# Copies of old cache rows issued in the last stage of a decoder step instead of the first

## The chip, the core and the metric

The kernel runs on one core of one Trainium2 chip. The metric is the device time of one execution in microseconds. Engines are named as in the profile: PE is TensorE, PEld its weight load, DVE is VectorE, ACT is ScalarE, POOL is GpSimd, SP is SyncE, which here only issues DMAs. HBM holds inputs and outputs.

## What is computed

One step of a decoder layer for a prompt of 2048 tokens and for 8 sequences of 4 new tokens each. The changed part is the last output of this cut of the reference: the rolling windows of keys and values, 2048 rows of 512 floats (2 KB) for each of 8 sequences. The first 2044 rows are old rows of the input, moved up by four; the last four are the new ones.

```
qa, ka, va, qb, kb, vb = project_qkv(rmsnorm(hs, norm_attn[l]), w_in[l], pos_s)
lb = state_win_k.shape[2]
k_all = jnp.concatenate([state_win_k[l], ka], axis=1)
v_all = jnp.concatenate([state_win_v[l], va], axis=1)
...
hs = hs + mix.astype(hs.dtype) @ w_out[l]
hs = mlp_sublayer(hs, norm_mlp[l], w_up[l], w_down[l])
...
wk_s.append(k_all[:, t:t + lb])
wv_s.append(v_all[:, t:t + lb])
```

Nothing in the kernel reads the old rows from the output: attention takes them from the input.

## The kernel before

Four stages run one after the other, each a block that all engines leave together through a barrier: `project`, `attend_prompt`, `attend_decode`, `mlp`. Every engine runs its own list of instructions in order, and semaphores tie the lists together.

**`project`** makes two passes (`h` = 0, 1) over 17 tiles of 128 tokens (the last has 32). Each pass has three column groups of the input weights in SBUF, split into a high and a low part, and each tile is multiplied three times per group (lines 398 to 400). For a tile, ACT squares `x` (line 253), DVE scales it by the root (line 303, which counts `xs_ready`), PE turns it (line 379) and multiplies, ACT copies the result, DVE rotates it (lines 345 to 350), PE turns it again (line 409), and ACT and DVE split the turned result (lines 287, 361). SP issues, in this order, the load of `x` for the tile after the next (line 164), the stores of keys and values (line 198), and four stores of 256 KB of the turned queries and keys (line 210: `qT_hi`, `qT_lo`, `kT_hi`, `kT_lo`). Between the passes SP loads the other three groups of weights (line 170), ACT casts them to the high part (line 263), and POOL subtracts to get the low part (line 239).

POOL also copies the old rows. `copy_window(n)` issues four DMAs from HBM to HBM for sequence `n`, a body of 2032 rows (4064 KB) and a rest of 12 rows, for keys and for values (lines 231, 233), once `xs_ready` has reached 3n + 5, so one sequence every three tiles. Four sequences come ahead of the subtractions of line 239, four behind them. POOL then waits for all of them.

**`attend_prompt`** and **`attend_decode`** are not touched. In `attend_decode` POOL issues 512 loads of cached values (line 843), among DVE's copies of turned keys (line 1086).

**`mlp`** goes over 5 blocks `b` of 416 tokens. A block first takes 8 column tiles of the output projection, then 16 groups `g` of hidden features. In a group PE multiplies two column tiles of the up weights, ACT and DVE apply the squared relu and split the result, and PE multiplies the down weights of the group before; DVE adds each of the eight results into `y` (line 1728), which frees one of three PSUM banks `d_dps`. All weights are read from HBM again for each block and split on the way: SP loads a tile to a raw buffer (line 1315 up, 512 KB; line 1320 down, 1024 KB), ACT casts it to the high part (lines 1514, 1520), and DVE subtracts (lines 1670, 1663). There are two raw buffers for up weights and one for down weights; DVE's subtraction lets SP issue the next load:

```
def load_rows(b, g):
    wait(sp, down_lo_ready, row_no(b, g))
    src = io["w_down"].rearrange("(g f p) n -> g p f n", p=P, f=NF)[g]
    sp.dma_start(down_raw[:], src).then_inc(down_in, 16)
```

Here `row_no(b, g)` is `b * 16 + g`. SP also loads the next block's mixed heads in some groups (line 1330) and stores the finished rows (line 1353). POOL has nothing to do in this stage.

Of the kernel before, what the change touches and what calls it, by code (L numbers as in the profile page):

```python
# [27 lines left out]
ND, TD = 8, 4  # L28
# [5 lines left out]
WIN = 2048  # L34
# [36 lines left out]
def project(nc, io, keep):  # L71
# [8 lines left out]
    NG, NR = 3, 2  # L80
# [3 lines left out]
    with ExitStack() as ctx:  # L84
        sb = lambda n, s, d=F32: ctx.enter_context(nc.sbuf_tensor(n, s, d))
        ps = lambda n: ctx.enter_context(nc.psum_tensor(n, [P, 512], F32))
        sem = lambda n: ctx.enter_context(nc.semaphore(n))
# [23 lines left out]
        w_ready = [sem(f"a_w_ready{i}") for i in range(2)]  # L111
# [4 lines left out]
        xs_ready = sem("a_xs_ready")  # L116
# [9 lines left out]
        stored = [sem(f"a_stored{b}") for b in range(2)]  # L126
        vec = sem("a_vec")
        VEC = 2 * NR + 1 + 2
        copied = sem("a_copied")

        w_cols = io["w_in"].rearrange("(c p) (g n) -> g p c n", p=P, n=GW)
        name = lambda h, i: GROUPS[i] + "ab"[h]
# [25 lines left out]
        with nc.Block() as block:  # L158
# [61 lines left out]
            @block.gpsimd  # L220
            def _(pool):

                body = (WIN - TD) // 16 * 16
                pool.wait_ge(w_ready[0], NG)

                def copy_window(n):
                    pool.wait_ge(xs_ready, n * 3 + 5)
                    for k in ("ka", "va"):
                        src = io[k + "_state"][bass.ds(n, 1)].rearrange("o t n -> (o t) n")
                        dst = io[k + "_win"][bass.ds(n, 1)].rearrange("o t n -> (o t) n")  # L230
                        pool.dma_start(dst[0:body].rearrange("(a b) n -> a b n", a=16),
                                       src[TD:TD + body].rearrange("(a b) n -> a b n", a=16)).then_inc(copied, 16)
                        pool.dma_start(dst[body:WIN - TD], src[TD + body:WIN]).then_inc(copied, 16)

                with pool.Fori(0, ND // 2) as n:
                    copy_window(n)
                for i in range(NG):
                    pool.wait_ge(w_hi_ready, NG + i + 1)
                    nc.gpsimd.tensor_tensor(w_lo[i][:], w_raw[(NG + i) % 2][:], w_hi[i][:].bitcast(F32),
                                            ALU.subtract).then_inc(w_ready[1], 1)  # L240
                with pool.Fori(ND // 2, ND) as n:
                    copy_window(n)
                pool.wait_ge(copied, 16 * 4 * ND)

            @block.scalar
            def _(act):
# [972 lines left out]
def mlp(nc, io, keep):  # L1219
# [3 lines left out]
    NB = (S + NS) // W  # L1223
# [3 lines left out]
    OG, UG = KC, FF // (NF * P)  # L1227
# [5 lines left out]
    with ExitStack() as ctx:  # L1233
        sb = lambda n, s, d=F32: ctx.enter_context(nc.sbuf_tensor(n, s, d))
        ps = lambda n: ctx.enter_context(nc.psum_tensor(n, [P, 512], F32))
        sem = lambda n: ctx.enter_context(nc.semaphore(n))
# [35 lines left out]
        down_hi_ready, down_lo_ready = sem("d_down_hi_ready"), sem("d_down_lo_ready")  # L1272
# [14 lines left out]
                                                   sem("d_y_rooted"))  # L1287
        y_ready = sem("d_y_ready")
        stored = [sem(f"d_stored{i}") for i in range(2)]
        vec = sem("d_vec")  # L1290

        out_no = lambda b, c: b * CG + c
# [12 lines left out]
        with nc.Block() as block:  # L1305
            @block.sync
            def _(sp):
# [77 lines left out]
                    put(LAST, t)  # L1385
                for i in range(2):
                    sp.wait_ge(stored[i], 16 * (NB * TB // 2 + (i == (NB * TB - 1) % 2)))

            def three(dst, w_hi, w_lo, x_hi, x_lo, first, last):

                nc.tensor.matmul(dst, w_hi, x_hi, start=first, stop=False)  # L1391
                nc.tensor.matmul(dst, w_hi, x_lo, start=False, stop=False)  # L1392
                return nc.tensor.matmul(dst, w_lo, x_hi, start=False, stop=last)  # L1393
# [400 lines left out]
def build(nc, io):  # L1794
    with ExitStack() as ctx:
        sb = lambda n, s: ctx.enter_context(nc.sbuf_tensor(n, s, F32))
        keep = {"ident": sb("ident", [P, P]), "qsT": sb("qsT", [P, 2 * NP, NS]), "ksT": sb("ksT", [P, 2 * NP, NS]),
                "mixsT": sb("mixsT", [P, 2 * NP, NS]), "neg_lam": sb("neg_lam", [P, 1])}
        for name in ("qT_hi", "qT_lo", "kT_hi", "kT_lo", "mixT"):
            io[name] = nc.dram_tensor(name, [2 * NP, P, S], F32, kind="Internal").ap()  # L1800
        project(nc, io, keep)
        attend_prompt(nc, io, keep)
        attend_decode(nc, io, keep)
        mlp(nc, io, keep)
# [91 lines left out]
```

## Time and profile before

| | before |
|---|---|
| median of 3 runs | 4207.3 us (4205.71 to 4209.13) |
| the profiled execution, own time | 4212.42 us |
| span of the profiled execution | 4210.9 us |
| granted clock of PE, mean | 0.961 |
| PE busy | 3851.8 us, 91% of the span |
| DVE busy | 2363.2 us, 56% |
| ACT busy | 1663.2 us, 39% |
| POOL busy | 921.5 us, 22% |
| DMA, mean | 172 GB/s, 722.35 MB in 493617 packets |
| `mlp`, from 2459 us on: PE busy | 1696.25 of 1752 us |
| `mlp`: DMA share, rate | 0.41, 123 GB/s |

The span runs from the first to the last instruction; the execution's own time has a little around it. Busy shares are means over stages with different limits, so each stage has to be read by itself. A granted clock of 1.00 is the upper of PE's two levels (2.4 GHz), 0.50 the lower (1.2 GHz). The DMA share is the mean busy share of the core's 16 DMA engines; it can come out a little over 1 in short stretches.

### The profile page before, as it was taken

To read this page: it belongs to the slowest core of one execution; us is meant where nothing else is said; L and a number is where in the kernel's file an instruction comes from. 1 tells how busy PE (TensorE), PEld (TensorE's weight loads), DVE (VectorE), ACT (ScalarE), POOL (GpSimd) and SP (SyncE) were. 2 spreads that over 40 slices of the span, in tenths; PEclk is the share of its full clock that TensorE was granted. 3 is DMA by queue.
4 is the path that set the end of the run, shared out by engine and by line. 5 is a ranking of instruction groups with operands and counts; after the bars stand their busy time and mean duration, and the time that the engine had idled before them with its cause. 6 is when DMAs were issued, how large, how long until landed. Compare 5 with 4: busy or idle time off the path is not lost. (4 is left out here: it accounts for less than half of the span.)

```text
span 4210.9 us, 72902 instructions
## 1 busy us (share of the span) xinstructions
PE 3851.8 (91%) x25066; PEld 3178.3 (75%) x25066; DVE 2363.2 (56%) x4793; ACT 1663.2 (39%) x2919; POOL 921.5 (22%) x784
## 2 busy tenths in 40 slices
PE   7997797999999978888888869999999999999998
PEld 6885685676777754444444549999999999999998
DVE  4344332555577854434434446666676676776765
ACT  2222121666666643222222234434444444443442
POOL 0002000988855543333333300000000000000000
PEclk9998998999999989989998979999999999999999
DMA  5776764111111129989989954334434433443432
GB/s 178 259 251 211 240 197 140 57 61 61 61 61 61 66 84 386 356 318 340 341 327 330 351 153 147 114 106 147 137 115 134 136 114 119 145 125 105 140 120 67
DMA packets 493617, 722.35 MB, mean 172 GB/s; under 512 B 30512, under 2 KB 331696, under 8 KB 487889
## 3 DMA queue, kind: packets, MB, share of 16 engines
q1 hardware_dynamic: 444841, 499.03, 36.5%
q0 software_dynamic: 47488, 218.01, 14.4%
q8 instruction: 191, 3.13, 0.3%
q14 instruction: 161, 1.32, 0.1%
q10 hardware_dynamic: 936, 0.86, 0.1%
HBM read 650.15 MB, written 134.48 MB: 186 GB/s over the span
## 5 line engine op out<-in xcount | busy, mean ns | idle before, releaser
L546 POOL TENSOR_SCALAR b_w<-b_w,b_inv 128x128 f32<-128x128 f32 (+7 forms) x192 | 578.9, 3025 | 425.8 <-DVE b_inv L698 255.4
L1728 DVE TENSOR_TENSOR d_y<-d_y,d_dps 128x416 f32<-128x416 f32 x640 | 372.2, 586 | 246.6 <-PE d_dps L1393 246.6
L1391 PE MATMUL d_dps<-d_u_hi,d_down_hi 128*128 128x416 f32 x1280 | 458.6, 358 | 11.4 <-DVE d_y L1728 11.4
L1393 PE MATMUL d_dps<-d_u_hi,d_down_lo 128*128 128x416 f32 x1280 | 453.1, 354 | 0.0
L1393 PE MATMUL d_ups<-d_h_hi,d_up_lo 128*128 128x416 f32 x1280 | 451.8, 353 | 0.0
L1391 PE MATMUL d_ups<-d_h_hi,d_up_hi 128*128 128x416 f32 x1280 | 449.9, 352 | 0.0
L1392 PE MATMUL d_dps<-d_u_lo,d_down_hi 128*128 128x416 f32 x1280 | 448.4, 350 | 0.0
L1392 PE MATMUL d_ups<-d_h_lo,d_up_hi 128*128 128x416 f32 x1280 | 446.7, 349 | 0.0
L898 PE MATMUL c_turn<-ident,c_k 128*128 128x128 f32 x2304 | 362.4, 297 | 69.5 <-ACT c_kT L1025 35.4
L898 PEld LDWEIGHTS c_turn<-ident,c_k 128*128 128x128 f32 x2304 | 262.0, 148 | 199.3 <-ACT c_kT L1025 88.0
L843 POOL DMA_DIRECT2D c_v<-in_v_cache x512 | 276.1, 539 | 596.2 <-issue 596.2
L622 ACT ACTIVATE b_w<-b_w,b_shift 128x128 f32<-128x128 f32 (+15 forms) x256 | 309.0, 1207 | 131.9 <-DVE b_shift L691 130.3
L398 PE MATMUL a_zps<-a_w_hi,a_xT_hi 128*128 128x512 f32 (+1 forms) x816 | 330.2, 405 | 10.6 <-DVE a_w_lo L331 7.5
L400 PE MATMUL a_zps<-a_w_hi,a_xT_lo 128*128 128x512 f32 (+1 forms) x816 | 326.7, 400 | 0.0
L399 PE MATMUL a_zps<-a_w_lo,a_xT_hi 128*128 128x512 f32 (+1 forms) x816 | 324.8, 398 | 0.0
L593 PE MATMUL b_ops<-b_wT,b_v 128*64 128x128 f32 (+1 forms) x3264 | 304.5, 282 | 21.9 <-ACT b_wT L634 17.4
L1086 DVE COPY c_kT<-c_turn 128x512 f32<-128x512 f32 x288 | 199.3, 692 | 202.8 <-PE c_turn L898 202.7
L1670 DVE TENSOR_TENSOR d_up_lo<-d_up_raw,d_up_hi 128x1024 fp32r<-128x1024 f32 x200 | 244.0, 1221 | 96.3 <-ACT d_up_hi L1514 96.2
L593 PEld LDWEIGHTS b_ops<-b_wT,b_v 128*64 128x64 f32 (+1 forms) x3264 | 250.8, 156 | 60.5 <-ACT b_wT L634 28.7
L1025 ACT COPY c_kT<-c_turn 128x512 f32<-128x512 f32 x288 | 168.7, 586 | 318.1 <-PE c_turn L898 318.1
L634 ACT COPY b_wT<-b_turn 128x512 f32<-128x512 f32 (+3 forms) x416 | 206.8, 522 | 156.0 <-PE b_turn L577 154.8
L577 PE MATMUL b_turn<-ident,b_w 128*128 128x128 f32 x1632 | 248.0, 285 | 18.0 <-POOL b_w L546 8.8
(188 smaller groups left out, 6849.9 us busy)
## 6 DMA issues: line engine op xcount, KB each, us to landing
c_k<-in_k_cache SPq DMA_DIRECT2D x512, 256.0 KB, 7.0
c_v<-in_v_cache POOLq DMA_DIRECT2D x512, 256.0 KB, 5.8
d_up_raw<-in_w_up SPq DMA_DIRECT2D x160, 512.0 KB, 4.2
d_down_raw<-in_w_down SPq DMA_DIRECT2D x80, 1024.0 KB, 5.5
out_ka_win<-in_ka_state POOLq DMA_DIRECT2D x8, 4064.0 KB, 15.8
out_va_win<-in_va_state POOLq DMA_DIRECT2D x8, 4064.0 KB, 27.6
d_up_raw<-in_w_out SPq DMA_DIRECT2D x40, 512.0 KB, 3.9
a_x<-in_x_prompt SPq DMA_DIRECT2D x32, 512.0 KB, 5.0
```

The source lines that it names most:

```text
L398: nc.tensor.matmul(dst, x_hi, w_hi[i][:, c, :], start=(c == 0), stop=False)
L399: nc.tensor.matmul(dst, x_hi, w_lo[i][:, c, :], start=False, stop=False)
L400: m = nc.tensor.matmul(dst, x_lo, w_hi[i][:, c, :], start=False, stop=(c == KC - 1))
L546: nc.gpsimd.tensor_scalar(row, row, inv[:, u % RB, m:m + 1], None, ALU.mult).then_inc(w_ready, 1)
L593: ins = nc.tensor.matmul(bank[h, at], v[i][:, kt, h], wT[copy_no(u, j, m) % WB][:, kt % 4 * P:(kt % 4 + 1) * P], start=(kt == 0), stop=(kt ...
L622: nc.scalar.activation(row, row, ACT.Exp, bias=shift[:, u % RB, m:m + 1], scale=-1.0, accum_out=total[:, u % RB, m:m + 1]).then_inc(exp_do ...
L843: eng.dma_start(dst[i][:, g, :], io[src[0]][bass.ds(page, 1)].rearrange("o p d -> (o p) d")).then_inc(landed[i], 16)
L898: last = nc.tensor.transpose(turn[e % 2][:, g * P:(g + 1) * P], k[i][:, half * 4 + g, p * P:(p + 1) * P], keep["ident"][:])
L1391: nc.tensor.matmul(dst, w_hi, x_hi, start=first, stop=False)
L1392: nc.tensor.matmul(dst, w_hi, x_lo, start=False, stop=False)
L1393: return nc.tensor.matmul(dst, w_lo, x_hi, start=False, stop=last)
L1728: nc.vector.tensor_tensor(part, part, d_ps[k % DB][:, 0:W], ALU.add).then_inc(d_used, 1)
```

## The change

The copies of the old rows leave `project`, and with them the counter `copied` and POOL's waits there. POOL gets a list in `mlp` instead. For each of the 80 groups (5 blocks of 16) it waits until DVE has split the group's down weights (`down_lo_ready`, line 1663 of the kernel before) and issues one copy of 400 rows (800 KB); behind every fifth piece it issues the remaining 44 rows of that window (88 KB). At the end POOL waits for all 96.

```diff
--- before.py
+++ after.py
@@ -126,7 +126,6 @@
         stored = [sem(f"a_stored{b}") for b in range(2)]
         vec = sem("a_vec")
         VEC = 2 * NR + 1 + 2
-        copied = sem("a_copied")
 
         w_cols = io["w_in"].rearrange("(c p) (g n) -> g p c n", p=P, n=GW)
         name = lambda h, i: GROUPS[i] + "ab"[h]
@@ -220,27 +219,10 @@
             @block.gpsimd
             def _(pool):
 
-                body = (WIN - TD) // 16 * 16
-                pool.wait_ge(w_ready[0], NG)
-
-                def copy_window(n):
-                    pool.wait_ge(xs_ready, n * 3 + 5)
-                    for k in ("ka", "va"):
-                        src = io[k + "_state"][bass.ds(n, 1)].rearrange("o t n -> (o t) n")
-                        dst = io[k + "_win"][bass.ds(n, 1)].rearrange("o t n -> (o t) n")
-                        pool.dma_start(dst[0:body].rearrange("(a b) n -> a b n", a=16),
-                                       src[TD:TD + body].rearrange("(a b) n -> a b n", a=16)).then_inc(copied, 16)
-                        pool.dma_start(dst[body:WIN - TD], src[TD + body:WIN]).then_inc(copied, 16)
-
-                with pool.Fori(0, ND // 2) as n:
-                    copy_window(n)
                 for i in range(NG):
                     pool.wait_ge(w_hi_ready, NG + i + 1)
                     nc.gpsimd.tensor_tensor(w_lo[i][:], w_raw[(NG + i) % 2][:], w_hi[i][:].bitcast(F32),
                                             ALU.subtract).then_inc(w_ready[1], 1)
-                with pool.Fori(ND // 2, ND) as n:
-                    copy_window(n)
-                pool.wait_ge(copied, 16 * 4 * ND)
 
             @block.scalar
             def _(act):
@@ -1287,6 +1269,7 @@
                                                    sem("d_y_rooted"))
         y_ready = sem("d_y_ready")
         stored = [sem(f"d_stored{i}") for i in range(2)]
+        rows_copied = sem("d_rows_copied")
         vec = sem("d_vec")
 
         out_no = lambda b, c: b * CG + c
@@ -1385,6 +1368,25 @@
                     put(LAST, t)
                 for i in range(2):
                     sp.wait_ge(stored[i], 16 * (NB * TB // 2 + (i == (NB * TB - 1) % 2)))
+
+            @block.gpsimd
+            def _(pool):
+
+                rows, pieces = 400, NB
+                rest = WIN - TD - rows * pieces
+                for n in range(NB * UG):
+                    pool.wait_ge(down_lo_ready, n + 1)
+                    who, k = n // pieces, n % pieces
+                    state = ("ka", "va")[who % 2]
+                    src, dst = io[state + "_state"][who // 2], io[state + "_win"][who // 2]
+                    at = slice(k * rows, (k + 1) * rows)
+                    old = slice(TD + k * rows, TD + (k + 1) * rows)
+                    pool.dma_start(dst[at].rearrange("(a b) n -> a b n", a=16),
+                                   src[old].rearrange("(a b) n -> a b n", a=16)).then_inc(rows_copied, 16)
+                    if k == pieces - 1:
+                        pool.dma_start(dst[WIN - TD - rest:WIN - TD].rearrange("(a b) n -> a b n", a=4),
+                                       src[WIN - rest:WIN].rearrange("(a b) n -> a b n", a=4)).then_inc(rows_copied, 16)
+                pool.wait_ge(rows_copied, 16 * (NB * UG + 2 * ND))
 
             def three(dst, w_hi, w_lo, x_hi, x_lo, first, last):
```

On POOL, in the projection, the order before was this (the three subtractions stand once, between two loops of four turns each):

```order
L235 ISA
L231 ISA [waits a_xs_ready]
L231 DMA out_ka_win<-in_ka_state 64x16256
L233 ISA
L233 DMA out_ka_win<-in_ka_state 16x384
L231 DMA out_va_win<-in_va_state 64x16256
L233 DMA out_va_win<-in_va_state 16x384
L235 REGISTER_ALU
L235 COMPARE_AND_BRANCH
L239 ISA
L239 TENSOR_TENSOR a_w_lo<-a_w_raw,a_w_hi 128x4096 [waits a_w_hi_ready] x3
L241 UNCONDITIONAL_BRANCH
```

and it is this now, in the numbering of the changed kernel:

```order
L219 UNCONDITIONAL_BRANCH [waits barrier_Pool_Activation_PE_DVE_SP_gather]
L224 ISA
L224 TENSOR_TENSOR a_w_lo<-a_w_raw,a_w_hi 128x4096 [waits a_w_hi_ready] x3
L157 UNCONDITIONAL_BRANCH
L521 UNCONDITIONAL_BRANCH [waits barrier_Pool_Activation_PE_DVE_SP_gather]
```

Only the subtractions are left between the two barriers; a body went out as 64 runs of 16256 floats.

On POOL, at the start of the last stage, where there was no row before, there now stands:

```order
L1372 UNCONDITIONAL_BRANCH [waits barrier_Pool_Activation_PE_DVE_SP_gather]
L1384 DMA out_ka_win<-in_ka_state 16x12800 [waits d_down_lo_ready] x5
L1387 DMA out_ka_win<-in_ka_state 16x1408
L1384 DMA out_va_win<-in_va_state 16x12800 [waits d_down_lo_ready] x5
L1387 DMA out_va_win<-in_va_state 16x1408
```

and so on for 16 windows: five pieces of 16 runs of 12800 floats, then a rest. The order of the instructions on PE, DVE, ACT and SP is the same as before.

## Rows read from the trace of the kernel before

**Rows 1.** Busy time by stretch: PE, PEld, DVE, ACT, POOL (instructions), granted clock, DMA share, GB/s.

```profile
250.00:300.00 50.00, 50.00 (x237) 40.82 (x236) 20.93 (x46) 11.49 (x23) 1.99 (x4) 1.00 0.86 283
...
400.00:450.00 50.00, 27.31 (x124) 22.25 (x123) 11.20 (x26) 4.48 (x9) 0.00 (x0) 0.80 0.96 316
450.00:500.00 50.00, 50.00 (x237) 40.82 (x236) 19.88 (x45) 11.38 (x23) 1.99 (x4) 1.00 0.69 229
```

**Rows 2.** Timeline of POOL, projection: start, us, operation, idle time before.

```profile
383.59 0.71 POOL L231 DMA_DIRECT2D out_ka_win<-in_ka_state  x1
...
397.10 0.50 POOL L231 DMA_DIRECT2D out_ka_win<-in_ka_state  x1 [11.33 <-DVE a_xs L303]
```

**Rows 3.** Timeline of SP's queue, projection, tiles with and without copies.

```profile
163.61 10.95 SPq L210 DMA_DIRECT2D kT_lo<-a_zT_lo  x1
...
394.93 23.76 SPq L210 DMA_DIRECT2D kT_hi<-a_zT_hi  x1
418.79 17.02 SPq L210 DMA_DIRECT2D kT_lo<-a_zT_lo  x1
436.07 2.46 SPq L164 DMA_DIRECT2D a_x<-in_x_prompt  x1
...
456.64 0.68 SPq L210 DMA_DIRECT2D kT_lo<-a_zT_lo  x1
```

**Rows 4.** Waits, 290 to 460 us: engine, what it waited for, sum, times, longest.

```profile
ACT a_xs L253 <- DMA a_x<-in_x_prompt: 31.3, 2, 30.5
```

**Rows 5.** Timeline of PE, first row after the stall.

```profile
445.65 1.75 PE L379 MATMUL a_turn<-ident,a_xs 128*128 128x128 f32 x7 [22.69 <-DVE a_xs L303]
```

**Rows 6.** Timeline of DVE, line 303, three tiles.

```profile
395.61 0.76 DVE L303 TENSOR_SCALAR a_xs<-a_x,a_stat 128x1024 f32<-128x1024 f32 x1
...
456.98 0.76 DVE L303 TENSOR_SCALAR a_xs<-a_x,a_stat 128x1024 f32<-128x1024 f32 x1
...
475.55 0.76 DVE L303 TENSOR_SCALAR a_xs<-a_x,a_stat 128x1024 f32<-128x1024 f32 x1
```

**Rows 7.** Busy time by stretch, just after the stall.

```profile
445.00:450.00 5.00, 4.35 (x17) 3.87 (x18) 4.35 (x11) 0.49 (x1) 0.00 (x0) 0.65 0.68 234
```

**Rows 8.** Source lines in the decode stage: min/median/max ns, first and last start.

```profile
L843 POOL DMA_DIRECT2D c_v<-in_v_cache x512: 538/539/601, 1566.2 to 2437.2; - x171
...
L1086 DVE COPY c_kT<-c_turn x288: 691/692/693, 1566.4 to 2439.2; 128x512 f32<-128x512 f32 x144
```

**Rows 9.** Page, part 6, DMA issues: KB each, median us to landing.

```profile
d_up_raw<-in_w_up SPq DMA_DIRECT2D x160, 512.0 KB, 4.2
d_down_raw<-in_w_down SPq DMA_DIRECT2D x80, 1024.0 KB, 5.5
...
out_va_win<-in_va_state POOLq DMA_DIRECT2D x8, 4064.0 KB, 27.6
```

**Rows 10.** Timelines of SP and of ACT in one group of the last stage.

```profile
3438.81 0.37 SPq L1315 DMA_DIRECT2D d_up_raw<-in_w_up  x1
3441.02 0.37 SPq L1320 DMA_DIRECT2D d_down_raw<-in_w_down  x1
...
3449.65 1.04 ACT L1514 CAST d_up_hi<-d_up_raw 128x1024 fp32r<-128x1024 f32 x1
3452.60 1.91 ACT L1520 CAST d_down_hi<-d_down_raw 128x2048 fp32r<-128x2048 f32 x1 [1.91 <-PE d_dps L1393]
```

**Rows 11.** Timeline of SP, a group that also loads the mix.

```profile
3250.70 0.37 SPq L1330 DMA_DIRECT2D d_mix<-mixT  x1
```

**Rows 12.** Busy time by stretch, the same group.

```profile
3240.00:3260.00 20.00, 20.00 (x103) 19.52 (x102) 13.65 (x21) 8.73 (x16) 0.00 (x0) 0.91 0.47 144
```

**Rows 13.** Waits of PE, last stage from 2560 us.

```profile
PE d_dps L1391 <- DVE d_y L1728: 11.4, 5, 2.6
```

**Rows 14.** Source line 345 on DVE: min/median/max ns.

```profile
L345 DVE TENSOR_TENSOR a_rot<-a_z,a_cos x68: 278/292/7061, 39.6 to 707.7; 128x128 f32<-128x128 f32 x64, 32x128 f32<-32x128 f32 x4
```

**Rows 15.** Timeline of DVE, the last split of down weights.

```profile
4167.63 2.29 DVE L1663 TENSOR_TENSOR d_down_lo<-d_down_raw,d_down_hi 128x2048 fp32r<-128x2048 f32 x1 [1.40 <-ACT d_down_hi L1520]
```

## The prediction

> **What bounds the kernel now.** I read the busy time by stretches first, since the change takes work out of one stage and puts it into another; then the waits and the timelines of the one stretch of the first stage in which TensorE stands idle while copies fly; then a group of the last stage, action by action. TensorE is the engine to look at in both stages.
>
> In the projection TensorE is busy for 50.00 of 50 us while the copies run beside it: from 250 to 300 us, with the DMA engines at a share of 0.86. The stretch from 400 to 450 us is different: 27.31 us busy, granted clock 0.80, and a DMA share of 0.96. From 450 us it is full again [rows 1]. So eight copies of K and eight of V cost this stage nothing most of the time, and something once.
>
> What happens there is a chain of five rows. POOL issues one pair of copies at 383.59 us and the next at 397.10 us, 13.5 us apart [rows 2], where the loops mean them to come three tiles apart. POOL had stood in the three subtractions of line 239 in between, so a pair that was due earlier came out late, just ahead of the next. With four bodies of 4064 KB on their way, SP's queue takes no more: the store of `kT_hi` sits 23.76 us in its issue and the one of `kT_lo` 17.02 us, where the latter takes 0.68 us with no copy in flight and 10.95 us beside one pair [rows 3]. Behind them in the same queue stands the load of `x` for the next tile; it is issued at 436.07 us. ScalarE's square of that tile waits 30.5 us for it [rows 4], and TensorE's turn of the tile is idle for 22.69 us [rows 5]. One pair at a time is absorbed, because the load is needed only a tile later; two are not.
>
> **The change, part by part.** *The copies leave the projection.* SP's stores are then issued in under 1 us each, as without a copy [rows 3], and the load of `x` goes out at about 396 us in place of 436 us, a whole tile before it is wanted. What that is worth comes from the pace of the tiles. Line 303 makes the normalized `x`, once a tile: at 395.61 us, then late, and two and three tiles on at 456.98 and 475.55 us [rows 6]. The steady distance is 475.55 - 456.98 = 18.57 us. Undisturbed, the start of 475.55 us would have stood at 395.61 + 3 x 18.57 = 451.32 us. The difference is **24.2 us**. A second way agrees: 22.69 us of idle time, and after it the clock is 0.65 for 4.35 us of work [rows 7], which loses (1 - 0.65) x 4.35 = 1.5 us, 24.2 together. TensorE also stands idle ahead of 383.59 us, during the reload of the weights and the subtractions on POOL; these stay, no copy flies beside them, and I count nothing for it. The gain reaches the end undiminished, as the later stages start at a barrier and depend on none of this.
>
> The largest that this term could be is ScalarE's whole wait, 30.5 us; the smallest is nothing, if the store queue were full for another reason.
>
> *POOL's wait for the copies at the end of the projection goes.* The last pair goes out when 7 x 3 + 5 = 26 of the 34 tiles have been normalized, eight tiles of 18.57 us before the stage's end, and lands in two. Worth nothing.
>
> *80 copies of 800 KB come into the last stage, and 16 rests of 88 KB.* POOL has no other work there, so its 96 issues (about 0.5 us each by the rows of the decode stage [rows 8]) delay nobody on POOL itself. The cost would be in what the transfers do to SP's weight loads. Two times 4064 KB are down 27.6 us after the second was issued [rows 9], so 800 KB are 800 / 8128 x 27.6 = 2.7 us of all DMA engines. A piece is let go by `down_lo_ready`, the same event that lets SP issue the next down weights, so the two do collide, in each of the 80 groups.
>
> The slack to set against it: in a typical group SP issues a load of up weights at 3438.81 us and one of down weights at 3441.02 us. They land after 4.2 and 5.5 us at the median [rows 9], so at 3443.0 and 3446.5 us. ScalarE casts these very tiles at 3449.65 and 3452.60 us, and the second cast waited for TensorE [rows 10]. So both have 6.1 to 6.6 us to spare, against 2.7 us (3.0 us where a rest follows). The second up load of the group has more. Nearest to the change there is a row that already does the like: at 3250.70 us SP adds an 832 KB load of `d_mix` to a group's own loads [rows 11], and TensorE is busy 20.00 of 20 us there [rows 12]. Over the whole of the stage from 2560 us on, TensorE's longest sum of waits is 11.4 us in five places, for additions on VectorE [rows 13]; no row there names a DMA. I take **0 us**. The bounds: nothing is won here by any row, as TensorE has no DMA wait to lose; on the other side I allow that the five waits for VectorE double, 11.4 us.
>
> *POOL's issue beside VectorE.* A copy is issued when line 1663 ends on VectorE, and line 1670 begins there at once. Rows of the decode stage: 512 POOL issues of 538 to 601 ns, and among them 288 copies on VectorE that took 691 to 693 ns, none of them stretched [rows 8]. But the row of line 345 shows that the two engines can block each other: 278 to 292 ns as a rule, and 7061 ns once, beside POOL's subtraction [rows 14]. I take the decode rows as the nearer ones, since a DMA issue is what POOL does here: 0 us. The Trainium skill ("SBUF — State Buffer", section "Who interferes with whom") says that VectorE and GpSimd share one pair of SBUF ports by an exclusive lock, that an instruction with two SBUF inputs contends with a GpSimd instruction that reads SBUF, and that the writing of descriptors can be shut out by some forms on VectorE. The trace agrees with the lock at line 345; for a DMA issue beside an instruction with two SBUF inputs no run here shows either. By that rule the sum would lie between this forecast and the first rival below.
>
> *The end.* The last piece is let go when the last line 1663 ends, at 4167.6 + 2.3 = 4169.9 us [rows 15], 41 us before the end of the span. Even with the 27.6 us of a whole copy in place of 3 us it would land before the last stores. The new wait at the end of POOL costs nothing.
>
> **The sum.** -24.2 + 0 + 0 + 0 = -24.2 us. The profiled execution took 4212.42 us around its span of 4210.9 us, 5.1 us above the median of 4207.3 us; its span should become about 4186.7 us. Taken off the median: 4207.3 - 24.2 = **4183 us**, 0.58% less. A measurement of this kernel tells about 0.2% from no change, 8.4 us.
>
> **Rivals.**
>
> *VectorE and POOL block each other in the last stage (slower).* Each of the 96 issues falls on an instruction of VectorE and holds it for about 0.5 us, and TensorE, which needs VectorE's additions to free its three `d_dps` banks, waits as long: 96 x 0.5 = 48 us, so 4183 + 48 = 4231 us. For it: line 345, and that VectorE's line 1670 starts just as POOL does. Against it: the 288 unstretched copies, and that VectorE is idle for 6.35 of 20 us even in a loaded stretch [rows 12], so that a delay of 0.5 us is made up within the group. It decides from the point where more than half of the 0.5 us reaches TensorE in each group (above 0.25 x 96 = 24 us the gain is gone).
>
> *The weight loads come late (slower).* If the copy's long runs pushed the loads back by the 10.95 us that one pair gave to `kT_lo` [rows 3], that is 10.95 - 6.6 = 4.3 us past the slack; times 80 it is 344 us, near 4530 us. It decides from a delay of over 6.6 us. Against it: that pair was ten times the bytes, and a piece of 2.7 us of service can't hold a queue for 11 us.
>
> *Nothing changes.* SP's queue was full of its own stores after the reload of the weights, the stall stays, and the time is 4207 us. For it: the stores come in a burst as TensorE starts again after the reload. Against it: the same store takes 0.68 us at a tile without copies and 10.95 us beside one pair [rows 3].
>
> That the change doesn't do what it says can be left aside: the rows of POOL's order show the copies gone from the first stage and 80 + 16 of them in the last.
>
> **How the numbers follow.** The forecast: 0.86. Nothing changes: 0.07. Blocked VectorE: 0.04. Late loads: 0.03. The forecast is the only case over 0.2% faster, the two slow ones are the slower cases: 0.86, 0.07, 0.07. The range is the forecast's own: down to the whole of ScalarE's wait (4207.3 - 30.5, about 4176), up to the doubled waits in the last stage (4183 + 11.4, about 4195). The 14% of the rivals and a little of the forecast's own lie outside.
>
> **What would show it.** Right: from 400 to 450 us TensorE is busy for 50 us at clock 1.00; SP's `kT_hi` and `kT_lo` issues are all below 1.5 us; the projection ends about 24 us earlier and the stages behind it keep their lengths; DMA share of the last stage goes from 0.4 to 0.5, and TensorE's waits there stay near 11 us. Wrong: a TensorE wait on `d_up_lo` or `d_down_lo`, a ScalarE wait for `d_up_raw` or `d_down_raw`, lines 1670 or 1728 (two lines further on in the new numbering) longer than before, or a `kT_hi` issue of tens of us that is still there.

## The result and the profile after

The changed kernel took **4183.5 us** (median of 5 runs, 4176.7 to 4189.8) against 4208.4 us for the kernel before (5 runs, 4205.7 to 4216.0): a ratio of 0.9938, 95% interval 0.992 to 0.9957. A repeat gave 0.9941 (0.9923 to 0.9959). The forecast was 4183 us, 0.9942. The profiled execution took 4177.45 us around its span of 4175.8 us.

First, the stretch of the projection in which TensorE stood idle. By stretches (columns as in [rows 1]):

```profile
250.00:300.00 50.00, 50.00 (x240) 40.90 (x239) 18.52 (x42) 11.75 (x24) 0.00 (x0) 1.00 0.38 113
400.00:450.00 50.00, 50.00 (x241) 40.94 (x241) 22.05 (x48) 11.37 (x23) 0.00 (x0) 1.00 0.33 104
450.00:500.00 50.00, 50.00 (x237) 40.85 (x236) 19.91 (x47) 9.15 (x18) 0.00 (x0) 1.00 0.35 111
```

And SP's queue at the tile that was stuck before:

```profile
392.74 0.41 SPq L209 DMA_DIRECT2D kT_hi<-a_zT_hi  x1
393.25 0.64 SPq L209 DMA_DIRECT2D kT_lo<-a_zT_lo  x1
394.15 0.66 SPq L163 DMA_DIRECT2D a_x<-in_x_prompt  x1
```

The two stores are issued in 0.41 and 0.64 us where they took 23.76 and 17.02 us [rows 3]; the load of `x` goes out at 394.15 us, where it went at 436.07 us. TensorE's 27.31 busy us of 50 [rows 1] are 50.00, at clock 1.00. Of TensorE's waits for line 303 (now 285) between 290 and 460 us, the 22.69 us [rows 5] are gone; one of 10.4 us stays, at the reload of the weights:

```profile
PE a_turn L361 <- DVE a_xs L285: 10.4, 1, 10.4
```

Second, the last stage, from the last matmul of the decode stage to the end of the span: 1751.8 us before, 1758.0 us after.

```profile
2417.80:4175.80 1758.00, 1698.52 (x9012) 1664.13 (x9012) 1171.92 (x1570) 726.78 (x1061) 46.74 (x96) 0.98 0.50 161
```

The same stretch before:

```profile
2459.10:4210.90 1751.80, 1696.15 (x9012) 1661.97 (x9012) 1171.71 (x1570) 726.08 (x1061) 0.00 (x0) 0.98 0.41 123
```

POOL's 96 issues are there and the DMA share went from 0.41 to 0.50, but the stage is 6.2 us longer. The transfers of the page (KB each, median us to landing):

```profile
d_up_raw<-in_w_up SPq DMA_DIRECT2D x160, 512.0 KB, 4.8
d_down_raw<-in_w_down SPq DMA_DIRECT2D x80, 1024.0 KB, 7.1
out_ka_win<-in_ka_state POOLq DMA_DIRECT2D x40, 800.0 KB, 6.9
out_va_win<-in_va_state POOLq DMA_DIRECT2D x40, 800.0 KB, 6.9
```

The weights land 0.6 and 1.6 us later than in [rows 9]. Two waits answer to [rows 13], here from 2520 us on; the second was not there before:

```profile
PE d_dps L1393 <- DVE d_y L1730: 14.4, 5, 3.7
ACT d_up_hi L1516 <- DMA d_up_raw<-in_w_up: 3.3, 4, 1.6
```

A fifth wait of ScalarE for these weights, 0.5 us, lies just ahead of 2520 us; so there is one at the start of each of the five blocks.

Where the time went, stage by stage in the profiles. The projection ends with TensorE's last turn of `z`, the second stage is from its first score to its last output matmul, the decode stage from its first turn of a key to its last `c_x` matmul, the last stage from there to the end of the span; the 18 to 20 us between the first and the second, and between the second and the third, are left out.

```
us                projection ends   second stage   decode   last stage   span
before                713.0            814.3        894.7     1751.8    4210.9
after                 686.7            811.1        882.5     1758.0    4175.8
after, repeat         686.6            809.4        878.1     1757.5    4169.1
before, repeat        711.1            814.0        901.0     1751.3    4216.1
```

The projection's end and the last stage move with the change and repeat within 2 us. The decode stage differs by 4 to 23 us between these four, though nothing in it was changed. So the difference of the two spans, 35.1 us, can't be read as the gain; the stages that the change touches give -26.3 + 6.2 = -20 us, and the medians -24.9 us.

### The profile page after: what moved, and what is told of

Its sections match the earlier page's. It is cut to its first block and busy times, and to the rows that moved or that the text cites. A ratio compares the mean times of both kernels' runs of the same rounds, so it can differ in the third digit from the quotient of the medians.

```text
span 4175.8 us, 72858 instructions
## 1 busy us (share of the span) xinstructions
PE 3846.3 (92%) x25066; PEld 3174.9 (76%) x25066; DVE 2363.1 (57%) x4793; ACT 1663.1 (40%) x2919; POOL 952.2 (23%) x848
## 5 line engine op out<-in xcount | busy, mean ns | idle before, releaser
L1393 PE MATMUL d_dps<-d_u_hi,d_down_hi 128*128 128x416 f32 x1280 | 459.7, 359 | 14.4 <-DVE d_y L1730 14.4
```

## The experiments

The theory, A in the texts on record: two pairs of copies in flight at once stop SP's queue, and this alone is the stall; in the last stage the copies are nearly covered. Its rivals are named in each text: that any copy in the projection costs, that nothing was gained there, that VectorE and POOL block each other in the last stage, or that the weight loads come late in every group. Each kernel was timed in rounds against the kernel before on the same chip; the ratios have 95% intervals.

**No copies at all.** From the changed kernel, the POOL block of `mlp` is taken out:

```diff
-            @block.gpsimd
-            def _(pool):
-
-                rows, pieces = 400, NB
...
-                pool.wait_ge(rows_copied, 16 * (NB * UG + 2 * ND))
```

> The changed kernel without the 96 copies in the last stage; the old rows of the windows are left out of the output. Theory A (the gain comes from the projection alone, and the copies in the last stage cost a few us at the five block starts): the projection as long as in the changed kernel (last turn of z at about 687 us), VectorE's additions hold TensorE up for 11.4 us in all in the last stage again (14.4 us with the copies), time 3 to 6 us below the changed kernel, 0.992 to 0.993 of the kernel before. Rival B (the copies cost nothing at all where they are now): the same time as the changed kernel, 0.994, and 14.4 us of waits stay.

Measured: 4174.4 us, ratio 0.9927 (0.9905 to 0.9949). The projection ends at 688.1 us and the last stage takes 1750.3 us. TensorE's five waits for `d_y` are down to 11.3 us, which speaks against rival B; the times alone can't tell the two apart. What the copies still cost in the changed kernel thus shows in the last stage, 6 to 8 us.

**Only the two pairs that collide.** From the kernel before, the first loop is taken out and the second issues two pairs; the other six are left out:

```diff
-                with pool.Fori(0, ND // 2) as n:
-                    copy_window(n)
...
-                with pool.Fori(ND // 2, ND) as n:
+                with pool.Fori(ND // 2, ND // 2 + 2) as n:
                     copy_window(n)
-                pool.wait_ge(copied, 16 * 4 * ND)
+                pool.wait_ge(copied, 16 * 4 * 2)
```

> The kernel before with only the fifth and sixth pair of copies left, issued behind the three subtractions as before; the other six sequences' old rows are left out of the output. Theory A (these two pairs, close together, make the whole stall): SP's kT_hi and kT_lo issues stay at 24 and 17 us, TensorE's wait for the turn stays at about 22.7 us, ratio to the kernel before 1.000 (within 0.002). Rival C (all copies slow the projection a little, and the stall is only a part): at least 5 us faster than the kernel before.

Measured: 4200.9 us, ratio 0.999 (0.9974 to 1.0007). The projection ends at 711.0 us. SP's queue, first the stuck stores:

```profile
392.92 23.71 SPq L210 DMA_DIRECT2D kT_hi<-a_zT_hi  x1
416.73 16.17 SPq L210 DMA_DIRECT2D kT_lo<-a_zT_lo  x1
433.15 2.46 SPq L164 DMA_DIRECT2D a_x<-in_x_prompt  x1
```

and TensorE's waits for line 301:

```profile
PE a_turn L377 <- DVE a_xs L301: 32.2, 2, 21.7
```

Two pairs of eight make the whole stall (the sum of 32.2 us holds the 10.4 us of the reload as well). The other six pairs add nothing to the projection's end: 711.0 us without them, 713.0 and 711.1 us with them. The times alone don't exclude rival C, as the interval reaches down to 0.9974, 11 us.

**All eight pairs, but kept apart.** From the kernel before; the second loop waits for one window's tiles more, so that the pair that POOL is late with doesn't meet the next:

```diff
-                def copy_window(n):
-                    pool.wait_ge(xs_ready, n * 3 + 5)
+                def copy_window(n, late=0):
+                    pool.wait_ge(xs_ready, n * 3 + (5 + late))
...
                 with pool.Fori(ND // 2, ND) as n:
-                    copy_window(n)
+                    copy_window(n, 3)
```

> The kernel before with all copies in the projection, but the last four pairs each wait for three more tiles, so that no two pairs are in flight together. Theory A: one pair is absorbed; no TensorE wait of over 15 us for the turn, the projection ends at about 689 us instead of 713 us, ratio to the kernel before 0.994 (24 us), and no cost in the last stage. Rival D (any copy in the second pass stalls SP's queue long enough to hold up the load of x): the stall stays or comes in another tile, gain under 8 us.

Measured: 4180.9 us, ratio 0.9949 (0.993 to 0.9967); the projection ends at 688.3 us. SP's queue beside the pair, and TensorE's stretch:

```profile
412.95 10.64 SPq L210 DMA_DIRECT2D kT_hi<-a_zT_hi  x1
423.70 0.88 SPq L210 DMA_DIRECT2D kT_lo<-a_zT_lo  x1
425.12 1.50 SPq L164 DMA_DIRECT2D a_x<-in_x_prompt  x1
```

```profile
400.00:450.00 50.00, 50.00 (x242) 40.96 (x241) 21.31 (x47) 11.04 (x21) 0.00 (x0) 1.00 0.73 242
```

One pair holds a store for 10.64 us, and TensorE doesn't notice. The fifth pair goes out later here too, at 396.71 us in place of 383.59 us, and no run leaves it alone at its old time. But in the kernel before it had landed by 413.1 us, and `kT_lo` sat in its issue from 418.79 to 435.81 us, until the sixth pair was nearly down (438.8 us); that part of the hold is the sixth pair's. The gain of the change can thus be had without moving a byte to another stage: three tiles more in the wait of four of the eight pairs. By the times the two kernels can't be told apart.

**The kernel before, again**, as a yardstick for the comparison, without an edit.

> The kernel before, unchanged, for a second profile. It tells how much each stage varies without a change. Theory A: projection, second stage and last stage within 2 us of the first profile; the decode stage, which moves over 300 GB/s and has TensorE below full clock, may vary by some 10 us. Rival E: the decode stage is the same to 2 us here, so the 12 us that it lost beside the change are an effect of the change.

Measured: 1.0001 (0.9982 to 1.0019). Its own runs spread by 0.7%, which sets what the times can tell. The decode stage took 901.0 us, 6.3 us more than in the first profile, and the other stages are within 2 us of it; so rival E falls.

**Pieces that keep away from a block's start.** From the changed kernel, the same 96 copies wait for other groups; a block's sixteen pieces go out from its third group on:

```diff
-                    pool.wait_ge(down_lo_ready, n + 1)
+                    pool.wait_ge(down_lo_ready, n // UG * UG + 2 + n % UG * (UG - 2) // UG + 1)
```

> The changed kernel, but no piece is issued in the first two groups of a block: the 16 pieces of a block go out in its groups 3 to 16, two of them in two of these groups. Theory A (the cost of the copies in the last stage is paid at the five block starts, where the up weights have no slack): TensorE's waits for VectorE's additions fall back to 11.4 us, ScalarE waits nowhere for d_up_raw in a group, the last stage is about 1752 us long (1758 us in the changed kernel), 4 to 6 us less than the changed kernel. Rival F (every group pays a little): the last stage stays at 1757 to 1759 us.

Measured: 4175.7 us, ratio 0.9936 (0.9915 to 0.9958). The last stage with the same issues and the same DMA share:

```profile
2428.20:4179.60 1751.40, 1695.63 (x9012) 1661.62 (x9012) 1171.37 (x1570) 725.96 (x1061) 46.52 (x96) 0.98 0.50 162
```

```profile
PE d_dps L1393 <- DVE d_y L1730: 11.3, 5, 2.6
```

The stage is back at 1751.4 us and the waits at about the 11.4 us of [rows 13]; ScalarE has no wait for `d_up_raw` left. So it is not the number of copies, not POOL's issues beside VectorE and not the bytes; it is where in the block they fall. The changed kernel and this one **again**, on one chip:

> The changed kernel, unchanged, for a second profile and more times. Theory A (the last stage pays about 6 us at the five block starts): the last stage 1757 to 1759 us again, ScalarE's wait for d_up_raw in four or five places; the projection 687 to 689 us; the decode stage anywhere from 875 to 900 us. Rival (the 6 us were chance): the last stage 1750 to 1754 us.

> The kernel whose pieces avoid the first two groups of each block, unchanged, on the same chip as the changed kernel of this call. Theory A: the last stage 1751 to 1753 us again; by the times 4 to 7 us (0.1 to 0.2%) below the changed kernel, less than the decode stage's own variation lets a few runs show. Rival: last stage as long as the changed kernel's.

Measured: 0.9941 (0.9923 to 0.9959) for the changed kernel, 0.9937 (0.9919 to 0.9954) for this one; last stages of 1757.5 and 1752.9 us. TensorE's waits repeat (14.4 and 11.3 us), and the stage differs again, by 4.6 us this time; the times can't confirm it.

**More of the same bytes.** From the changed kernel, each piece is copied once more (then three times more) into a scratch tensor in DRAM:

```diff
+                scratch = nc.dram_tensor("scratch", [1, 2 * ND, WIN, GW], F32, kind="Internal").ap()
...
+                    for more in range(1):
+                        pool.dma_start(scratch[more, who, at].rearrange("(a b) n -> a b n", a=16),
+                                       src[old].rearrange("(a b) n -> a b n", a=16)).then_inc(rows_copied, 16)
...
```

> The changed kernel, but each piece is copied a second time, into a scratch tensor in HBM: 1600 KB per group, 5.4 us of all DMA engines. Theory A: 5.4 us are still below the 6.1 us to spare in a steady group, so only the block starts get worse: about 3 us more at each of five, the last stage 1765 to 1775 us. Rival F (every group pays in proportion): about as much again as the copies cost now, 1764 us. Rival G (the loads are late in every group as soon as copies take this long): 80 x 1 us or more, over 1830 us.

> As the double one, with each piece copied four times: 3200 KB per group, 10.9 us of all DMA engines beside some 8 us of weight loads in a group of 18 us. Theory A: past the 6.1 us to spare and at the limit of the DMA engines; every group is late, by 1 to 5 us, the last stage 1830 to 2150 us. Rival F: 1782 us (four times 6 us, and a little). Rival H (the queue with the smaller packets always gets its turn, so that loads stay on time whatever POOL copies): under 1770 us, the copies finish late.

Measured: 0.9986 (0.9966 to 1.0005) with twice the bytes, 1.0191 (1.015 to 1.0231) with four times; last stages of 1773.2 and 1867.4 us, so 22 and 116 us above a stage without copies, where the change costs 6. Waits of the first, then of the second kernel:

```profile
PE d_dps L1397 <- DVE d_y L1734: 25.8, 5, 5.6
ACT d_down_hi L1526 <- DMA d_down_raw<-in_w_down: 23.2, 5, 6.4
ACT d_up_hi L1520 <- DMA d_up_raw<-in_w_up: 12.4, 4, 3.6
```

```profile
ACT d_down_hi L1526 <- DMA d_down_raw<-in_w_down: 128.6, 29, 9.4
ACT d_up_hi L1520 <- DMA d_up_raw<-in_w_up: 120.2, 21, 19.2
PE d_dps L1397 <- DVE d_y L1734: 113.5, 12, 21.2
```

With twice the bytes TensorE waits at the five block starts only, as theory A has it; ScalarE's five waits for down weights lie in other groups and don't reach TensorE. At four times the bytes ScalarE is late for weights 50 times, yet TensorE waits 12 times, and the five waits at block starts (20.80, 20.33, 20.31, 20.57 and 21.21 us) make 103.2 of the 113.5 us. The groups in between still have cover for most of it, at four times the load. So this stage is inside theory A's range, but not for theory A's reason, that every group is late. Rivals F, G and H fall.

**The copies in the second stage.** That stage moves 11 to 108 GB/s by the page's slices, so SP could issue the copies there in half windows of 2016 KB, one behind each store of its 32 results, with POOL's block of the last stage taken out:

```diff
+                def copy_rows(g):
+                    who, half = g // 2, g % 2
...
+                    rows = 1008
...
+                    sp.dma_start(dst[at].rearrange("(a b) n -> a b n", a=48),
+                                 src[old].rearrange("(a b) n -> a b n", a=48)).then_inc(rows_copied, 16)
...
                 for g in range(NU // OT):
                     put(g)
+                    copy_rows(g)
...
+                sp.wait_ge(rows_copied, 16 * (4 * ND + 2 * ND))
```

> No copies in the first and in the last stage; SP issues them in the second stage instead, half a window (2016 KB) behind each of the 32 stores of mixed heads, and the rests of 28 rows behind every second one. DMA engines are at a share of 0.1 to 0.2 there, and SP's loads there are fetched a pair of heads ahead. Theory A: the projection as in the changed kernel (687 us), the second stage within 3 us of it (811 us), the last stage 1751 us: 6 us below the changed kernel, ratio to the kernel before 0.992 to 0.993. Rival I (SP's stores of mixed heads or its loads wait behind the copies and hold TensorE up): the second stage 10 us or more longer.

Measured: 4189.7 us, ratio 0.9966 (0.995 to 0.9982), a miss. The projection (689.9), the second stage (813.5) and the last stage (1753.2) are as they should be, but between the second stage and the decode stage TensorE stands for 26.1 us in place of 18.6 to 19.7 in the others. The last half window goes out just before the stage's end, and there SP waits for the copies (the last line of the edit): the last of them lands at 1532.38 us, the last store of mixed heads at 1525.88 us. So SP comes to the barrier 6.5 us later, and the first load behind it comes late (waits, this kernel and the kernel before):

```profile
DVE c_q_rows L1069 <- DMA c_v_new<-out_vb_s: 33.2, 1, 33.2
```

```profile
DVE c_q_rows L1070 <- DMA c_v_new<-out_vb_s: 25.8, 1, 25.8
```

These 7 us are less than half of the 15 to 19 us by which the time lies above theory A's; the rest was not pinned down.

**The same, done earlier**: no copy behind the last four stores, two behind four early ones.

```diff
-                    copy_rows(g)
+                    for _ in range((g < 28) + (g in (5, 9, 13, 17))):
+                        copy_rows(next_half.pop(0))
```

> The copies in the second stage on SP again, but none behind the last four of the 32 stores: 28 stores are followed by one half window and four of these by a second. Theory A (the copy behind the last store made the stage end late, 26.1 us from the last product to the first turn of the decode stage where the changed kernel has 19.0 us): 19 to 20 us there, the second stage 810 to 815 us, the last stage 1751 to 1753 us, ratio to the kernel before 0.992 to 0.995. Rival (the second stage is slowed all along): the stage stays 813 us or longer and the gap stays above 24 us.

Measured: 4180.1 us, ratio 0.9933 (0.9915 to 0.9952). The gap is 18.9 us again, and the wait is back:

```profile
DVE c_q_rows L1071 <- DMA c_v_new<-out_vb_s: 26.0, 1, 26.0
```

This kernel, the spaced pairs and the late pieces are each as fast as the changed kernel, and none is faster by more than the intervals.

## Why the prediction was right, and where it was off

**The stall: right.** 24.2 us were forecast. By the end of the projection the change is worth 24.4 us (711.1 to 686.7) to 26.4 us (713.0 to 686.6), and kernels without two pairs in flight end it between 686.6 and 690.1 us. Each link was tested by itself: with only the two pairs that meet, all of the stall is there; with eight pairs apart, none. That SP's queue was full of its own stores, the rival in which nothing changes, falls with both. The 2 to 3.5 us by which these ends differ among themselves belong to something else: the first 50 us of the projection, where no copy flies yet, differ from profile to profile. From the fifth start of line 303 (near 88 us) to the projection's end it is 623.3 and 622.9 us before, 600.1 and 599.9 us after. Counted so, the change is worth 22.8 to 23.4 us, about 1 us less than forecast.

**The last stage: 0 forecast, 6.2 us measured.** The step that failed is "in a typical group ... both have 6.1 to 6.6 us to spare". In a typical group, 18 to 19 us from the next, that holds for the up weights. For the down weights the prediction took the median of 5.5 us; the very load that it shows landed after 7.46 us and had 4.1 us to spare. That is still more than 2.7 us, and even fourfold bytes leave TensorE undisturbed in most of those groups. But the first groups of each of the five blocks come closer: no down product of an earlier group lies between them. POOL's rows, about 19 us apart elsewhere, show it:

```profile
3528.14 0.49 POOL L1384 DMA_DIRECT2D out_va_win<-in_va_state  x1 [72.73 <-DVE d_down_lo L1665]
3537.64 0.49 POOL L1384 DMA_DIRECT2D out_va_win<-in_va_state  x1 [9.01 <-DVE d_down_lo L1665]
...
3557.60 0.49 POOL L1384 DMA_DIRECT2D out_ka_win<-in_ka_state  x1 [18.99 <-DVE d_down_lo L1665]
```

In the kernel before, at the same start, the up weights issued at 3567.51 us (the row merges two loads, this is the first) were cast at 3574.42 us:

```profile
3567.51 5.86 SPq L1315 DMA_DIRECT2D d_up_raw<-in_w_up  x2
```

```profile
3574.42 1.03 ACT L1514 CAST d_up_hi<-d_up_raw 128x1024 fp32r<-128x1024 f32 x1
```

That is 6.9 us. How long the up weights of this start took to land, in the kernel before and in the changed one, stands at the end of the view of their tile:

```profile
DMA to landing us min/median/max: 4.1/4.9/6.6
```

```profile
DMA to landing us min/median/max: 4.2/5.4/8.6
```

So 0.3 us were to spare before, not 6. After the change the load issued at 3529.02 us, 0.9 us behind a piece, took the 8.6 us, and ScalarE waited for it (SP's row, ScalarE's, then TensorE's behind it):

```profile
3529.02 5.86 SPq L1298 DMA_DIRECT2D d_up_raw<-in_w_up  x2
```

```profile
3537.67 1.05 ACT L1516 CAST d_up_hi<-d_up_raw 128x1024 fp32r<-128x1024 f32 x1 [1.65 <-DMA d_up_raw<-in_w_up]
```

```profile
3543.23 0.57 PE L1393 MATMUL d_dps<-d_u_hi,d_down_hi 128*128 128x416 f32 x1 [3.67 <-DVE d_y L1730]
```

2.0 us later landing, less 0.3 us of slack, is 1.7 us; the wait is 1.65 us, and TensorE's goes from 2.18 to 3.67 us. The delay by a piece was sized well (2.7 us of service forecast, 2.0 us of delay here); the slack was read in the wrong group. With the pieces kept away from the start, the slowest load lands after 6.6 us again and TensorE's wait is 2.18 us.

Matched instruction by instruction with the kernel before, TensorE falls back by 1.83, 0.39, 0.35, 3.11 and 0.37 us around the five starts, 6.05 of the 6.2 us. The waits make 14.4 - 11.4 = 3.0 us of it. The rest is in the first and the fourth start, and goes with the clock. Busy time of the 5 us behind the waits of these two, after:

```profile
2522.45:2527.45 5.00, 5.00 (x18) 4.83 (x19) 2.76 (x5) 0.97 (x2) 0.00 (x0) 0.66 0.80 263
...
3543.23:3548.23 5.00, 5.00 (x20) 4.73 (x21) 2.59 (x5) 1.29 (x5) 0.00 (x0) 0.66 0.40 123
```

and before:

```profile
2563.03:2568.03 5.00, 5.00 (x26) 4.81 (x27) 3.34 (x7) 0.97 (x2) 0.00 (x0) 1.00 0.88 280
...
3580.23:3585.23 5.00, 5.00 (x28) 4.91 (x29) 3.26 (x6) 1.30 (x5) 0.00 (x0) 1.00 0.39 112
```

After, all five such stretches are granted 0.66, in the repeat too; before, three of five are, in the repeat too (the two that are not are shown). A mean of 0.66 says that part of the stretch ran at 1.2 GHz in place of 2.4. By estimate, two more such stretches lose 2 x 5 x (1 - 0.66) = 3.4 us, and 3.0 + 3.4 = 6.4 us against the 6.2 measured. The longer wait is not all that decides on the clock: with late pieces, where the waits are as before, the clock is below 1.00 at three starts in one profile and at four in the other. Of the nine profiles without a piece at a block's start, the seven with three such starts have a last stage of 1750.3 to 1751.8 us, the two with four 1752.9 and 1753.2 us. That the copies make it five rests on the two profiles of the changed kernel. The doubled waits that the range allowed, 11.4 us, covered it.

**The rival of late weight loads** was thus true in kind: its sign, a wait of ScalarE for `d_up_raw`, is in the profile. It was wrong in place and size: five starts in place of 80 groups, 6 us in place of 344.

**The rival of VectorE and POOL falls.** Lines 1672 after and 1670 before, ns at least, in the middle and at most:

```profile
L1672 DVE TENSOR_TENSOR d_up_lo<-d_up_raw,d_up_hi x200: 1211/1219/1227, 2437.0 to 4119.0; 128x1024 fp32r<-128x1024 f32 x100
L1384 POOL DMA_DIRECT2D out_ka_win<-in_ka_state x40: 488/488/520, 2508.5 to 4044.5; - x40
```

```profile
L1670 DVE TENSOR_TENSOR d_up_lo<-d_up_raw,d_up_hi x200: 1211/1219/1227, 2477.9 to 4154.1; 128x1024 fp32r<-128x1024 f32 x100
```

Not one instruction of this line is longer, although it has two inputs in SBUF and 48 of POOL's 96 issues run beside it. The late pieces, with all 96 issues, cost the stage nothing. On the lock of the ports that the Trainium skill describes ("SBUF — State Buffer", section "Who interferes with whom"), the trace shows it for POOL's subtraction [rows 14] and shows no trace of it for an issue of a copy. The prediction drew too much from that section: by it an instruction with two SBUF inputs contends with a GpSimd instruction that reads SBUF, not with one that only writes it, and it infers that the writing of descriptors needs the write side. The trace agrees with that.

**"The gain reaches the end undiminished": not shown as finely as it was put.** No stage behind the projection got longer by its removal, but the decode stage took 873 to 901 us over the thirteen profiles. So the agreement of 4183.5 with 4183 is closer than its parts: about -23 us in the projection, counted from the fifth start of line 303, and +6 us in the last stage make some -17 us, and the medians fell by 24.9 us. The remaining 8 us are within what the untouched stages move by and were not pinned down. That they cover the term of 6 us that was put at nothing is luck.

## What to carry to other kernels

Copies behind an engine that stands in other work come out in a bunch, and here the bunch, not the bytes, held up another queue: look first whether they can be kept apart where they are. Before laying a transfer beside loads, read the slack at the tightest group of the stage (the first of a block, where groups stand closer), not at a typical one, and issue nothing just ahead of a barrier that the barrier then has to wait for. Read such changes by stages: an untouched stage that wobbles by 28 us hides a term of 6 us in the total time.

## What was not expected

The decode stage, at 334 to 344 GB/s and with nothing in it changed, took 873.2 to 882.5 us in the four profiles of kernels that issue a piece in every group (the changed kernel, its repeat, and the two with more bytes) and 882.1 to 901.1 us in the nine others, although it ends before the first piece is issued. With mostly one profile per kernel this may be chance; if it is not, it would explain why late pieces gain 6 us in the last stage and nothing in the time. No run here tells these apart.

The cost of bytes in the last stage is far from proportional: 6, 22 and 116 us above the stage without copies for one, two and four times the bytes, with the DMA share at 0.50, 0.59 and 0.76 of the whole stage.
